# Causal and neighbourhood attention: two softmax blocks added, transposed once, and masked apart again

## The chip, the cores and the metric

The kernel runs on one core of a Trainium2 chip. The metric is the time of one execution on the device in microseconds; of the kernel before, three runs gave 1100.22, 1100.55 and 1100.86 us (median 1100.55).

## The reference, cut to what matters

Three layers work on a sequence of 512 tokens with 1024 channels, all in float32: a recurrent layer (RG-LRU), a layer of causal sliding-window attention, and a block that runs two attentions side by side (a two-sided window and a neighbourhood on an 8 x 64 grid) ahead of an MLP. The causal one and the neighbourhood one are touched here.

```python
def sliding_window_sink_attention(q, k, v, sinks):      # 16 heads, 2 key heads, WINDOW = BLOCK = 128
    # each block of 128 queries sees the block of keys before it and its own
    dist = (jnp.arange(BLOCK)[:, None] + BLOCK) - jnp.arange(2 * BLOCK)[None, :]
    valid = (dist >= 0)[None] & (dist < WINDOW)[None] & (abs_k >= 0)
    s = jnp.where(valid, s + alibi, -jnp.inf)
    ...
    p = (p / denom); o = einsum('bnkgqs,bnskd->bnqkgd', p, vb)

def neighborhood_attn(q, k, v, rpb):                    # 8 heads, grid of 8 rows x 64 columns
    col_start = jnp.clip(cols - B_KW // 2, 0, GRID_W - B_KW)      # each column sees 16 columns, all 8 rows
    ...
    p = softmax(scores + bias); out = einsum(p, v)
```

In the causal attention a query at place q of its block sees key k of the block before only if k > q, and key k of its own block only if k <= q. So for each query each of the 128 places is seen in exactly one of the two blocks. In the neighbourhood attention, with 16 columns seen and the grid cut into blocks of 16 columns, the same holds column by column, except that for the queries at the two edges of the grid one block is seen whole and the other not at all.

## The kernel before, in words

Activations lie as 128 channels by 512 tokens. All large products run on TensorE as a stream of tiles of 128 x 128 weights against 512 tokens. A float32 product is made of three matmuls of a narrower kind: weights and activations are each split into a high and a low part (ScalarE makes the high part of a weight unit of eight tiles, L1094, and VectorE the low part `wl`, L1414). One tile, three matmuls (L900 to L902), is the unit of time, a tick, in which the whole program is ordered: every piece of work on every engine is a generator that yields the tick at which it wants to be issued, and `merge` writes each engine's pieces out in the order of these ticks. The ticks fix only the order; when something really runs is up to the semaphores it waits for. An engine runs its list strictly in order, so that an instruction that waits holds up all behind it.

Attention is cut into 32 jobs of four heads (or of two heads and two query blocks): 16 causal jobs `s`, 8 windowed jobs `w`, 8 neighbourhood jobs `n`. They are threaded into the projections: `s` into the projection that makes queries and gates of the second layer, `w` and `n` into those of the last block. `SETS` (L552) holds each kind's first tick and the ticks per unit of work, and `plan_steps` (L558) lays out steps. In step n TensorE does the products of job n-3 (`prods`, L1055 or L1049), the scores of job n (L1009) and the turns of job n-2 (L1024), in this order; between the steps run projection tiles. A causal step with two blocks in all its parts is 0.84 x 8 = 6.72 ticks wide, a neighbourhood step 1.6 x 8 = 12.8.

A job of kind `s` or `n` with two key blocks runs like this. VectorE adds the bias to the scores of each of the four heads, with the minimum of the row (`biases`, L1682 for `s`, L1691 for `n`); ScalarE takes the exponential with its sum, in place in a tile `Pt` of 128 queries x 256 keys (L1298); VectorE adds the sink's term and takes the reciprocal (L1711, L1714; L1700 for `n`); GpSimd multiplies the tile by it (`normals`, L1958). TensorE transposes each 128 x 128 half of the four tiles into one PSUM bank, a turn of four transposes for each key block (`turns`). A turn is copied to SBUF (a tile `PT` of 128 keys x 4 x 128 queries) by VectorE if its number is even (L1728) and by ScalarE if it is odd (L1315), both placed 0.2 ticks behind the turn; then `prods` multiplies it with the values. The first causal block has only one key block: 4 of the 16 causal jobs. The next job's scores wait until VectorE has done all four biases of the job before (`bias_done`). Windowed jobs have two or three key blocks that overlap in their places.

Behind the causal stage, `y_mix` (L1651), `y_high` (L1286) and the low part (L1656) build the gated output for the next projection, placed by `y_tick` (L672); the silu of the gates (L1645) runs beside the attention.

Of the kernel before, what the change touches and what calls it, by code (L numbers as in the profile page):

```python
# [279 lines left out]
def build(nc, xT, wst, wcr, par, cst, nbias, wdn, fin, out):  # L280
    ctx = ExitStack()
    with ctx:
        def sem(n):
            return ctx.enter_context(nc.semaphore(n))
# [21 lines left out]
        sums_r = [sb(n, [128, 128], R)[:, :] for n in ("ones_r", "hones_r")]  # L306
        crossw = sb("crossw", [128, 4, 4, 32])
# [94 lines left out]
        fin_in, cross_in, cross_half = sem("fin_in"), sem("cross_in"), sem("cross_half")  # L402

# [123 lines left out]

        def unit_split(q, v):

            q.wait_ge(hi_done, v + 2)  # L530
            q.wait_ge(lo_done, v + 2)
# [3 lines left out]
        jobs, t_no = [], 0  # L535
# [16 lines left out]
        SETS = {"s": (0, 16, A_END + 44.5, 0.84), "w": (16, 24, B_END + 50.3, 1.22), "n": (24, 32, B_END + 145.3, 1.6)}  # L552
# [5 lines left out]
        def plan_steps(kind):  # L558

            a, z, tick, step = SETS[kind]
            at = {}
            for n in range(a, z + 3):
                n_prod = jobs[n - 3]["nk"] if n >= a + 3 else 0
                n_turn = jobs[n - 2]["nk"] if a + 2 <= n < z + 2 else 0
                wide = step * max(5.5 if n < z and kind != "n" else 0, (4 if n < z else 0) + n_turn + n_prod)
                for kb in range(n_prod):
                    at["prod", n - 3, kb] = tick
                for i in range(4 if n < z else 0):  # L570
                    at["score", n, i] = tick + (0.5 * wide if kind == "w" and i > 1 else 0.0)
                for kb in range(n_turn):
# [128 lines left out]
        def _(e):  # L701
# [81 lines left out]
            merge([weights(), starts(), biases(), swaps(), downs(), gains(), stores()])  # L783
# [3 lines left out]
        def _(e):  # L787
# [282 lines left out]
        def _(e):  # L1070
# [205 lines left out]
            def silu_b(c):  # L1276
                yield ev_at["bq", 8 + c] + 0.8
                q.wait_ge(ev_done, ev_no(("bq", 8 + c)))
                q.wait_ge(silu2_done, c - 1)
                e.activation(th_b[c % 2], gu_b[c % 2], ACT.Tanh, scale=0.5).then_inc(th_done, 1)  # L1280

            def y_high(c):
                yield y_tick(c) + 1.0
# [22 lines left out]
            def turn_copies(kind):  # L1306
                for m in range(*SETS[kind][:2]):
                    for kb in range(jobs[m]["nk"]):
                        t = jobs[m]["t0"] + kb
                        if t % 2:  # L1310
                            yield step_at["turn", m, kb] + 0.2
                            o, ring = t_tile(m, kb)
                            q.wait_ge(turn_done, t + 1)
                            q.wait_ge(prod_done, t - ring + 1)
                            e.activation(o, bank[TB[t % 2]], ACT.Copy).then_inc(pta_done, 1)  # L1315
# [82 lines left out]
        def _(e):  # L1398
# [239 lines left out]
            def silu_b(c):  # L1638
# [3 lines left out]
                yield ev_at["bq", 8 + c] + 1.9  # L1642
# [15 lines left out]
            def biases(kind):  # L1658
                for m in range(*SETS[kind][:2]):
                    job = jobs[m]  # L1660
                    w = 128 * job["nk"]
                    for i in range(4):
                        yield score_tick(m, i) + 0.4
# [8 lines left out]
                        if old >= 4 * (0 if kind == "s" else 16):  # L1672
                            o = jobs[old // 4]
                            q.wait_ge(turn_done, o["t0"] + o["nk"])
# [18 lines left out]
                        if i % 2:  # L1693
                            pair = 2 * m + i // 2
                            rd = stat_(m, 3, i - 1, i + 1)
                            if kind == "n":
                                yield score_tick(m, i) + 1.35
# [10 lines left out]
                            yield score_tick(m, i) + 1.35  # L1708
# [10 lines left out]
            def turn_copies(kind):  # L1719
                for m in range(*SETS[kind][:2]):  # L1720
                    for kb in range(jobs[m]["nk"]):
                        t = jobs[m]["t0"] + kb
                        if t % 2 == 0:
                            yield step_at["turn", m, kb] + 0.2
                            o, ring = t_tile(m, kb)
                            q.wait_ge(turn_done, t + 1)
                            q.wait_ge(prod_done, t - ring + 1)
                            e.tensor_copy(o, bank[TB[t % 2]]).then_inc(ptd_done, 1)  # L1728
# [188 lines left out]
        def _(e):  # L1917
# [31 lines left out]

            def normals(kind):  # L1950
                for m in range(*SETS[kind][:2]):
                    w = 128 * jobs[m]["nk"]
                    for i in range(4):
                        yield score_tick(m, i | 1) + 1.6
                        q.wait_ge(rd_done, 2 * m + i // 2 + 1)
                        q.wait_ge(exp_done, 4 * m + i + 1)
                        pm = p_tile(m, i)[0][:, 0:w]
# [17 lines left out]
            lanes += [normals(kind) for kind in SETS]  # L1975
# [163 lines left out]

# [23 lines left out]
```

## Time and profile before

| | |
|---|---|
| median of three runs | 1100.55 us |
| the profiled execution | 1100.17 us |
| its span | 1098.4 us |
| TensorE busy | 1087.8 us, 99% |
| VectorE busy | 753.4 us, 69% |
| ScalarE busy | 551.7 us, 50% |
| GpSimd busy | 121.4 us, 11% |
| granted clock of TensorE | 0.998 of full speed |

The span is from the first to the last instruction; the execution's own time is 1.8 us longer. TensorE's matmuls overlap in the records, so their mean length (390 ns for one of 512 columns) is more than each takes from the stream. The causal stage lies at about 265 to 385 us of the span, the windowed one at 462 to 560 us, the neighbourhood one at 563 to 657 us.

### The profile page before, as it was taken

The numbers are of one execution on the slowest core, as the hardware profiler recorded it, in microseconds if no ns is written. First come the engines' busy times: TensorE is split into PE (matmuls) and PEld (weight loads), VectorE is DVE, ScalarE is ACT, GpSimd is POOL, SyncE is SP. The second block draws the span as 40 slices with busy tenths as digits, with TensorE's granted clock in tenths as the row PEclk, the third lists the DMA queues.
The fourth block names the chain that finished last, engine by engine and source line by source line (L and its number), as shares of the span: only waits on it lengthen the run. The fifth ranks groups of instructions, "written<-read, shape, count | busy, mean of one in ns | idle before, by whom it ended". The sixth has DMA issues, their size and how long they took to land.

```text
span 1098.4 us, 14327 instructions
## 1 busy us (share of the span) xinstructions
PE 1087.8 (99%) x5216; PEld 863.0 (79%) x5216; DVE 753.4 (69%) x1274; ACT 551.7 (50%) x939; POOL 121.4 (11%) x170
## 2 busy tenths in 40 slices
PE   9999999999999999999999999999999999999997
PEld 6787787887677788767778788888888888888886
DVE  7898886777668765365545545546697796796795
ACT  6766656565666544244444433335553453453455
POOL 2000000120223311032112110003000000000003
PEclk9999999999999999999999999999999999999999
DMA  6322322332111222311322212323501702602401
GB/s 232 127 77 96 96 84 70 116 115 87 58 43 67 65 81 96 102 65 63 104 72 100 77 60 96 105 89 121 204 20 60 266 1 74 233 1 84 166 1 77
DMA packets 29910, 103.01 MB, mean 94 GB/s; under 512 B 3472, under 2 KB 3856, under 8 KB 29840
## 3 DMA queue, kind: packets, MB, share of 16 engines
q1 hardware_dynamic: 29408, 101.47, 27.1%
q8 instruction: 42, 0.69, 0.3%
q10 hardware_dynamic: 432, 0.62, 0.2%
q14 instruction: 28, 0.23, 0.1%
HBM read 99.45 MB, written 2.10 MB: 92 GB/s over the span
## 4 chain that ended last, share of the span: by engine, by line
PE 97%; DVE 1%; issue 0%; ACT 0%; POOL 0%; DVEq 0%; POOLq 0%
PE ps L900 24%; PE ps L901 24%; PE ps L902 24%; PE ps L864 4%; PE ps L863 4%; PE ps L865 4%; PE ps L1009 3%; PE ps L1024 3%; PE ps L1055 2%; PE ps L813 1%; PE ps L1049 1%; PE ps L946 0%; PE ps L938 0%; PE ps L965 0%; PE ps L975 0%
## 5 line engine op out<-in xcount | busy, mean ns | idle before, releaser
L900 PE MATMUL ps<-xgh,wh 128*128 128x512 f32 x847 | 336.8, 398 | 1.7 <-ACT trr L1184 0.8
L902 PE MATMUL ps<-xgh,wl 128*128 128x512 f32 x847 | 330.2, 390 | 0.0
L901 PE MATMUL ps<-xgl,wh 128*128 128x512 f32 x847 | 330.0, 390 | 0.0
L1414 DVE TENSOR_TENSOR wl<-raw,wh 128x1024 fp32r<-128x1024 f32 x146 | 186.3, 1277 | 44.4 <-ACT wh L1094 43.7
L1094 ACT ACTIVATE wh<-raw 128x1024 fp32r<-128x1024 f32 x146 | 153.0, 1050 | 78.7 <-PE ps L902 58.2
L900 PEld LDWEIGHTS ps<-xgh,wh 128*128 128x128 f32 x847 | 159.0, 188 | 40.8 <-issue 6.4
L902 PEld LDWEIGHTS ps<-xgh,wl 128*128 128x128 f32 x847 | 159.0, 188 | 33.8
L901 PEld LDWEIGHTS ps<-xgl,wh 128*128 128x128 f32 x847 | 159.2, 188 | 32.2 <-issue 1.0
L1958 POOL TENSOR_SCALAR Pt<-Pt,stat 128x256 f32<-128x256 f32 (+2 forms) x128 | 74.0, 590 | 275.8 <-DVE stat L1714 200.3
L1298 ACT ACTIVATE Pt<-Pt,stat 128x256 f32<-128x256 f32 (+2 forms) x128 | 64.3, 503 | 60.5 <-DVE stat L1682 23.1
L863 PE MATMUL ps<-wh,fh 128*128 128x512 f32 x224 | 87.1, 389 | 0.0
L864 PE MATMUL ps<-wl,fh 128*128 128x512 f32 x224 | 87.1, 389 | 0.0
L865 PE MATMUL ps<-wh,fl 128*128 128x512 f32 x224 | 87.1, 389 | 0.0
L1094 ACT ACTIVATE wh<-b 128x1024 fp32r<-128x1024 f32 x40 | 42.3, 1060 | 50.5 <-PE ps L865 40.5
L1315 ACT ACTIVATE PT<-ps 128x512 f32<-128x512 f32 x32 | 19.1, 597 | 80.2 <-PE ps L1024 80.1
L1890 DVE TENSOR_TENSOR xtok<-ps,xtok 128x512 f32<-128x512 f32 x56 | 38.0, 685 | 26.2 <-PE ps L865 26.2
L1728 DVE COPY PT<-ps 128x512 f32<-128x512 f32 x32 | 22.1, 690 | 49.3 <-PE ps L1024 49.0
L865 PEld LDWEIGHTS ps<-wh,fl 128*128 128x128 f32 x224 | 42.0, 188 | 8.8
L863 PEld LDWEIGHTS ps<-wh,fh 128*128 128x128 f32 x224 | 42.0, 188 | 8.8
L864 PEld LDWEIGHTS ps<-wl,fh 128*128 128x128 f32 x224 | 42.0, 188 | 8.7
L1414 DVE TENSOR_TENSOR wl<-b,wh 128x1024 fp32r<-128x1024 f32 x40 | 48.3, 1215 | 0.1
L1363 ACT ACTIVATE fa<-rl 128x512 f32<-128x512 f32 x32 | 20.1, 627 | 43.1 <-DVE rl L1835 43.1
(239 smaller groups left out, 1656.1 us busy)
## 6 DMA issues: line engine op xcount, KB each, us to landing
raw<-wst SPq DMA_DIRECT2D x146, 512.0 KB, 3.5
b<-wdn SPq DMA_DIRECT2D x32, 512.0 KB, 6.9
bst<-nbias SPq DMA_DIRECT2D x8, 256.0 KB, 3.3
xt<-xT SPq DMA_DIRECT2D x3, 512.0 KB, 7.8
outT<-xtok SPq DMA_DIRECT2D x3, 512.0 KB, 2.6
sq<-fin SPq DMA_DIRECT2D x2, 256.0 KB, 4.3
cstt<-cst SPq DMA_DIRECT2D x1, 448.0 KB, 5.6
raw<-wst SPq DMA_DIRECT2D x1, 320.0 KB, 5.0
```

The source lines that it names most:

```text
L863: e.matmul(o, a, high, start=(k == 0 and not on), stop=False, skip_group_check=on)
L864: e.matmul(o, a, low, start=False, stop=False, skip_group_check=on)
L865: e.matmul(o, b, high, start=False, stop=stop, skip_group_check=on).then_inc(tile_done, 1)
L900: e.matmul(o, high, a, start=(k == 0), stop=False)
L901: e.matmul(o, high, b, start=False, stop=False)
L902: done = e.matmul(o, low, a, start=False, stop=stop)
L1009: e.matmul(score_place(m, i + p), own, seen, start=True, stop=True).then_inc(score_done, 1)
L1094: e.activation(wh_t[:, v % NHL, :], src, ACT.Copy).then_inc(hi_done, 1)
L1298: e.activation(pa, pa, ACT.Exp, scale=-1.0, bias=stat_(m, 0, i, i + 1), accum_out=stat_(m, 1, i, i + 1)).then_inc(exp_done, 1)
L1414: e.tensor_tensor(wl_t[:, v % NHL, :], src, f32(wh_t[:, v % NHL, :]), ALU.subtract).then_inc(lo_done, 1)
L1890: e.tensor_tensor(x_, bank[ch.bank[name]], x_, ALU.add).then_inc(ev_done, 1)
L1958: e.tensor_scalar(pm, pm, stat_(m, 3, i, i + 1), 1.0, ALU.mult, ALU.mult).then_inc(nrm_done, 1)
```

## The change: what it does

For causal jobs with two blocks and for all neighbourhood jobs (`packed`), GpSimd adds the two halves of each `Pt` tile after the exponential (masked places are exactly zero there), normalises 128 columns instead of 256, and TensorE turns the sum once. The two blocks are got back on the keys' side by multiplying the turned tile with two complementary masks of 0 and 1, which come from the host and lie in the room of `crossw`, 256 KB each for the causal and for the neighbourhood kind.

For the neighbourhood jobs VectorE makes both masked tiles straight from PSUM. For the causal jobs ScalarE copies the turned bank to the second tile, VectorE multiplies that into the first tile with the first mask, and when it has, GpSimd multiplies the second tile in place with the other. Jobs that aren't packed are copied as before. Several places in the order move: copies from 0.2 to 1.0 ticks behind the turn, biases 0.4 ticks earlier, reciprocals from 1.35 to 2.15, normalisations from 1.6 to 2.4, the silu and the mixing of the causal stage, and the windowed set from `B_END + 50.3` with 1.22 to `B_END + 52.3` with 1.28. The width of a step still counts both blocks as turns.

```diff
+            job["packed"] = job["kind"] == "n" or (job["kind"] == "s" and job["nk"] == 2)
+            job["turns"] = 1 if job["packed"] else job["nk"]
...
-        SETS = {"s": (0, 16, A_END + 44.5, 0.84), "w": (16, 24, B_END + 50.3, 1.22), "n": (24, 32, B_END + 145.3, 1.6)}
+        SETS = {"s": (0, 16, A_END + 44.5, 0.84), "w": (16, 24, B_END + 52.3, 1.28), "n": (24, 32, B_END + 145.3, 1.6)}
...
-            return max(ev_at["bq", 8 + c] + 2.4, done[c // 4] + 1.4 + (1.1 if c > 3 else 6.0) * (c % 4))
+            return max(ev_at["bq", 8 + c] + 2.4, done[c // 4] + 3.4 + (1.1 if c > 3 else 4.0) * (c % 4))
...
+            def attention_masks():
+                yield end["gi", 11] + 4.0
+                q.wait_ge(tile_done, end["gi", 11] + 1)
+                e.dma_start(masks[:, :, :, :], msk[0]).then_inc(mask_in, 16)
+                yield end["z", 5]
+                copy_done(q, copied[15, 0])
+                if 15 in masked:
+                    q.wait_ge(mask_done, masked[15])
+                q.wait_ge(tile_done, B_END)
+                e.dma_start(masks[:, :, :, :], msk[1]).then_inc(mask_in, 16)
...
             def turns(kind):
                 for m in range(*SETS[kind][:2]):
                     job = jobs[m]
-                    for kb in range(job["nk"]):
+                    for kb in range(job["turns"]):
                         yield step_at["turn", m, kb]
-                        t = job["t0"] + kb
-                        q.wait_ge(pta_done if t % 2 else ptd_done, t // 2)
+                        t = job["u0"] + kb
+                        if t > 1:
+                            copy_done(q, bank_read[t - 2])
...
-                        q.wait_ge(pta_done if t % 2 else ptd_done, t // 2 + 1)
+                        copy_done(q, copied[m, kb])
+                        if kb and m in masked:
+                            q.wait_ge(mask_done, masked[m])
...
-                            yield step_at["turn", m, kb] + 0.2
+                            yield step_at["turn", m, 0 if packed else kb] + 1.0
                             o, ring = t_tile(m, kb)
...
-                            e.activation(o, bank[TB[t % 2]], ACT.Copy).then_inc(pta_done, 1)
+                            e.activation(o, bank[TB[u % 2]], ACT.Copy).then_inc(pta_done, 1)
...
-                        yield score_tick(m, i) + 0.4
+                        yield score_tick(m, i) + 0.0
...
-                            yield score_tick(m, i) + 1.35
+                            yield score_tick(m, i) + 2.15
...
+                        yield step_at["turn", m, 0 if packed else kb] + (2.6 if packed else 1.0)
...
+                        turned = bank[TB[u % 2]]
+                        if m in masked:
+                            copy_done(q, copied[m, 1])
+                            turned = t_tile(m, 1)[0]
...
+                            wide, seen = "p (b q) -> p b q", masks[:, kb, 0, :].unsqueeze(1).to_broadcast([128, 4, 128])
+                            e.tensor_tensor(o.rearrange(wide, b=4), turned.rearrange(wide, b=4), seen,
+                                            ALU.mult).then_inc(ptd_done, 1)
...
+            def packs(kind):
+                for m in range(*SETS[kind][:2]):
+                    for i in range(4 if jobs[m]["packed"] else 0):
+                        yield score_tick(m, i) + 1.9
+                        q.wait_ge(exp_done, 4 * m + i + 1)
+                        pm = p_tile(m, i)[0]
+                        e.tensor_tensor(pm[:, 0:128], pm[:, 0:128], pm[:, 128:256], ALU.add).then_inc(pack_done, 1)
+
+            def second_masks(kind):
+                for m in range(*SETS[kind][:2]):
+                    if m in masked:
+                        yield step_at["turn", m, 0] + 2.0
+                        o = t_tile(m, 1)[0]
+                        copy_done(q, copied[m, 1])
+                        copy_done(q, copied[m, 0])
+                        q.wait_ge(mask_in, 16 if kind == "s" else 32)
...
+                            o = o.rearrange(wide, b=4)
+                        e.tensor_tensor(o, o, seen, ALU.mult).then_inc(mask_done, 1)
+
             def normals(kind):
                 for m in range(*SETS[kind][:2]):
-                    w = 128 * jobs[m]["nk"]
+                    w = 128 * jobs[m]["turns"]
                     for i in range(4):
-                        yield score_tick(m, i | 1) + 1.6
+                        yield score_tick(m, i | 1) + 2.4
```

## Rows read from the trace of the kernel before

**Rows 1.** The page: busy time of each engine, then the chain's shares by engine.
```profile
PE 1087.8 (99%) x5216; PEld 863.0 (79%) x5216; DVE 753.4 (69%) x1274; ACT 551.7 (50%) x939; POOL 121.4 (11%) x170
...
PE 97%; DVE 1%; issue 0%; ACT 0%; POOL 0%; DVEq 0%; POOLq 0%
```

**Rows 2.** Waits of TensorE, 265 to 386 us: total us, times, longest.
```profile
PE ps L1009 <- DVE stat L1682: 0.6, 1, 0.6
```

**Rows 3.** Groups by line and form, TensorE: count, busy us, mean ns, idle before.
```profile
L1024 PE MATMUL ps<-cstt,Pt 128*128 128x128 f32 x256 | 35.9, 280 | 0.0
```

**Rows 4.** The chain in order of time, causal stage: start us, us, what.
```profile
335.01 0.59 PE ps L1024 x4
...
345.36 0.58 PE ps L1055 x4
...
354.22 1.02 PE ps L1024 x8
...
355.25 0.23 PE ps L900
...
360.04 1.01 PE ps L1055 x8
...
380.95 1.02 PE ps L1024 x8
...
384.05 1.01 PE ps L1055 x8
```

**Rows 5.** The chain in order of time, neighbourhood stage.
```profile
585.08 1.02 PE ps L1024 x8
```

**Rows 6.** Groups by line and form, VectorE and ScalarE, 240 to 386 us.
```profile
L1414 DVE TENSOR_TENSOR wl<-raw,wh 128x1024 fp32r<-128x1024 f32 x17 | 20.8, 1221 | 1.0 <-ACT wh L1094 0.8
...
L1656 DVE TENSOR_TENSOR y2l<-sgt,y2h 128x512 fp32r<-128x512 f32 x4 | 2.8, 689 | 0.2 <-ACT y2h L1286 0.2
...
L1315 ACT ACTIVATE PT<-ps 128x512 f32<-128x512 f32 x14 | 8.3, 596 | 17.0 <-PE ps L1024 16.9
```

**Rows 7.** GpSimd's operations: two lines' durations (ns min/median/max), and one in order of time.
```profile
L1948 POOL TENSOR_TENSOR ssq<-ssq,sq x21: 1325/1342/1853, 210.0 to 764.6; 128x512 f32<-128x512 f32 x21
...
L1958 POOL TENSOR_SCALAR Pt<-Pt,stat x64: 365/478/1891, 269.0 to 376.9; 128x256 f32<-128x256 f32 x48, 128x128 f32<-128x128 f32 x16
...
396.34 0.65 POOL L1945 TENSOR_SCALAR ssq<-sq 128x512 f32<-128x512 f32 x1 [18.49 <-ACT sq L1228]
```

**Rows 8.** Busy us (xcount) by stretch: length, PE, PEld, DVE, ACT, POOL; clock, DMA.
```profile
345.30:375.10 29.80, 29.80 (x173) 22.07 (x172) 23.16 (x74) 19.09 (x56) 11.88 (x17) 1.00 0.18 60
...
265.00:385.00 120.00, 119.30 (x672) 86.34 (x671) 84.98 (x285) 76.01 (x221) 34.95 (x64) 1.00 0.18 58
560.00:680.00 120.00, 120.00 (x673) 96.03 (x672) 60.73 (x138) 51.47 (x108) 17.67 (x32) 1.00 0.25 84
```

**Rows 9.** DMA issues: count, KB each, us from issue to landing.
```profile
crossw<-wcr SPq DMA_DIRECT2D x1, 256.0 KB, 4.3
```

**Rows 10.** VectorE in order of time, a dense causal step: start us, us, instruction.
```profile
358.19 0.16 DVE L1711 TENSOR_TENSOR stat<-stat 128x2 f32<-128x2 f32 x1 [0.69 <-ACT stat L1304]
...
359.58 0.47 DVE L1682 CUSTOM_DVE_ANT_0 Pt<-ps,cstt,drv 128x256 f32<-128x256 f32 x1
359.99 0.07 DVE L1682 DVE_READ_ACCUMULATOR2_ANT stat<- 128x1 f32 x1
```

**Rows 11.** VectorE and GpSimd in order of time, two places.
```profile
353.50 1.20 DVE L1414 TENSOR_TENSOR wl<-raw,wh 128x1024 fp32r<-128x1024 f32 x1
354.62 0.68 DVE L1656 TENSOR_TENSOR y2l<-sgt,y2h 128x512 fp32r<-128x512 f32 x1
...
353.67 2.34 POOL L1958 TENSOR_SCALAR Pt<-Pt,stat 128x256 f32<-128x256 f32 x2 [1.27 <-DVE stat L1714]
...
398.98 1.32 POOL L1948 TENSOR_TENSOR ssq<-ssq,sq 128x512 f32<-128x512 f32 x1 [1.99 <-ACT sq L1228]
...
399.08 2.31 DVE L1414 TENSOR_TENSOR wl<-raw,wh 128x1024 fp32r<-128x1024 f32 x1
```

More of the change, by code:

```diff
@@ L526, in form_no_, with copy_done @@
             return n + ({"A11": 1, "A": 2, "S": 3} if k == KH - 1 else {"A11": 1, "A": 1, "S": 2})[part]
+        def copy_done(q, which):
+            q.wait_ge(pta_done if which[0] == "act" else ptd_done, which[1])
         def unit_split(q, v):
@@ L534, in build @@
         D1, D2 = C_("D1"), C_("D2")
-        jobs, t_no = [], 0
+        jobs, t_no, u_no, pack_no = [], 0, 0, 0
+        copies, copied, bank_read = {"act": 0, "dve": 0}, {}, {}
+        masked, masks_no, SHARED = {}, 0, ('s',)
         for g in range(2):
@@ L551, in build @@
             t_no += job["nk"]
-        SETS = {"s": (0, 16, A_END + 44.5, 0.84), "w": (16, 24, B_END + 50.3, 1.22), "n": (24, 32, B_END + 145.3, 1.6)}
+            job["packed"] = job["kind"] == "n" or (job["kind"] == "s" and job["nk"] == 2)
+            job["turns"] = 1 if job["packed"] else job["nk"]
+            job["u0"], job["packs"] = u_no, pack_no
+            u_no += job["turns"]
+            pack_no += 4 * job["packed"]
+            for kb in range(job["nk"]):
+                u = job["u0"] + (0 if job["packed"] else kb)
+                by = ("dve", "act")[kb if job["packed"] and job["kind"] in SHARED else 0 if job["packed"] else u % 2]
+                copies[by] += 1
+                copied[m, kb] = (by, copies[by])
+                if by == "act" or not (job["packed"] and job["kind"] in SHARED):
+                    bank_read[u] = copied[m, kb]
+                if job["packed"] and by == "act":
+                    masked[m] = masks_no = masks_no + 1
+        SETS = {"s": (0, 16, A_END + 44.5, 0.84), "w": (16, 24, B_END + 52.3, 1.28), "n": (24, 32, B_END + 145.3, 1.6)}
         def head(job, i):
@@ L571, in plan_steps @@
                     at["score", n, i] = tick + (0.5 * wide if kind == "w" and i > 1 else 0.0)
-                for kb in range(n_turn):
+                for kb in range(jobs[n - 2]["turns"] if n_turn else 0):
                     at["turn", n - 2, kb] = tick + (0.5 * wide if kb > 1 else 0.0)
@@ L781, in stores @@
                 q.wait_ge(out_done, 16 * 5)
-            merge([weights(), starts(), biases(), swaps(), downs(), gains(), stores()])
+            merge([weights(), starts(), attention_masks(), biases(), swaps(), downs(), gains(), stores()])
         @block.tensor
@@ L1673, in biases @@
                             o = jobs[old // 4]
[L1674 removed]
+                            q.wait_ge(turn_done, o["u0"] + o["turns"])
                         if m >= 2:
@@ L1722, in turn_copies @@
                         t = jobs[m]["t0"] + kb
[L1723 to L1728, printed above, removed]
+                        if copied[m, kb][0] == "act":
+                            continue
+                        packed = jobs[m]["packed"]
+                        yield step_at["turn", m, 0 if packed else kb] + (2.6 if packed else 1.0)
+                        o, ring = t_tile(m, kb)
+                        u = jobs[m]["u0"] + (0 if packed else kb)
+                        q.wait_ge(turn_done, u + 1)
+                        q.wait_ge(prod_done, t - ring + 1)
+                        if not packed:
+                            e.tensor_copy(o, bank[TB[u % 2]]).then_inc(ptd_done, 1)
+                            continue
+                        q.wait_ge(mask_in, 16 if kind == "s" else 32)
[3 more added lines that the diff above has]
+                            turned = t_tile(m, 1)[0]
+                        if kind == "n" and jobs[m]["half"]:
+                            wide, seen = "p (a b q) -> p a b q", masks[:, kb, :, :].unsqueeze(2).to_broadcast([128, 2, 2, 128])
+                            e.tensor_tensor(o.rearrange(wide, a=2, b=2), turned.rearrange(wide, a=2, b=2), seen,
+                                            ALU.mult).then_inc(ptd_done, 1)
+                        else:
+                            wide, seen = "p (b q) -> p b q", masks[:, kb, 0, :].unsqueeze(1).to_broadcast([128, 4, 128])
+                            e.tensor_tensor(o.rearrange(wide, b=4), turned.rearrange(wide, b=4), seen,
+                                            ALU.mult).then_inc(ptd_done, 1)
             def key_a():
@@ L2137, in neighbour_bias, with attention_masks @@
     return full
+def attention_masks():
+    key, own = np.arange(128)[:, None], np.arange(128)[None, :]
+    first = np.stack([np.stack([key > own] * 2), np.stack([key % 16 >= own % 16, (own % 16 < 8) & (key >= 0)])])
+    both = np.stack([first, ~first], axis=1)
+    return np.ascontiguousarray(both.transpose(0, 3, 1, 2, 4).astype(np.float32))
 def kernel(**inputs):
```

31 lines of the change are left out of this document (23 added, 8 removed).

## The prediction

> **What bounds the kernel now.** I read the page first: TensorE is busy in 99% of the span and holds 97% of the chain that ended last [rows 1]. So the end moves when TensorE's own stream gets shorter or when TensorE is made to wait, and by nothing else. Next the list of TensorE's waits: in the attention stages it waits once, 0.6 us, for VectorE's bias step at L1682 [rows 2]; every other hand-over arrives in time. Then the group of the transposes, x256 [rows 3], and the chain in order of time, because groups of matmuls overlap in the busy rows and the chain gives what each really takes from the stream: a run of eight transposes 1.02 us, a run of four 0.59 us, one matmul of the projections 0.23 us [rows 4]. A tick of the written order is one projection tile, three matmuls, 0.69 us.
>
> **What is removed from TensorE.** A turn is four transposes of one 128-key block. Twelve of the sixteen causal jobs (all but the first block's four) and all eight neighbourhood jobs have two blocks; each now has one turn. That is 20 turns, 80 of the 256 transposes. Every such run goes from eight to four: 1.02 - 0.59 = 0.43 us, in the causal stage [rows 4] and the same in the neighbourhood stage [rows 5]. 20 x 0.43 = 8.6 us. The total of the group bounds it from above: 35.9 us / 256 x 80 = 11.2 us [rows 3], but that busy time overlaps its neighbours. The lower bound is 0, if TensorE had been waiting anyway and the wait only grew; with one wait of 0.6 us in the stage [rows 2] that is far off. I take 8.6, measured on the same runs of four and eight. Scores and products stay as they are.
>
> **What is added elsewhere, and what hides it.**
> ScalarE and VectorE in the causal stage: 14 copies each before; after, ScalarE makes 12 + 2 and VectorE 12 masks + 2 copies. A copy on ScalarE is 0.60 us; a VectorE product of 128x512 with both inputs in SBUF is 0.69 us [rows 6], what its copies cost too, so neither engine's load changes by itself.
> GpSimd in the causal stage: 48 sums of 128x128, 12 masks of 128x512, and 48 normalisations at half the width. The mask has a row: 1.34 us [rows 7]. The sum has none. Bounds: 0.37 us (the shortest one-input operation, the 128-wide one) and 1.34 us. The second input of a 128x512 operation costs 1.34 - 0.65 = 0.69 us [rows 7], a quarter of it 0.17, so I take 0.37 + 0.17 = 0.54 us. The normalisation falls from 0.48 (median) to 0.37. A causal step gains 4 x 0.54 + 1.34 - 4 x 0.11 = 3.1 us of GpSimd. In the four steps of 345.3 to 375.1 it was busy 11.9 of 29.8 us [rows 8]; it becomes some 24 of 28.
> Neighbourhood stage: VectorE masks both tiles straight from PSUM, 16 operations for 8 copies, +8 x 0.69 = 5.5 us; it was busy 60.7 of 120 us there [rows 8] and a step holds 12.8 ticks, 8.8 us of tiles. ScalarE loses 8 copies. GpSimd gets 4 x 0.54 a step. TensorE needs the masked tiles a step later, 8.8 us, against 1.4 us for two masks. Cost 0; without that cover it would be 1.4 us a step.
> Two loads of masks, 256 KB each: a load of this size landed in 4.3 us [rows 9]. The first is issued on SyncE behind the last cross gates' tile, 128 ticks (88 us) before the causal stage begins; the weights queued behind it are asked for 40 tiles (27 us) ahead of use. Cost 0; uncovered, 4.3 us each.
> Windowed attention: no work changes; its set starts 2 ticks later with 5% longer steps, so that its last products come 6.3 ticks later, still 6 ticks (4.3 us) ahead of the first tile that reads them, and the copy and the low part after them take 0.60 + 0.69 us. Cost 0, at most 1 us. The widths of the causal and neighbourhood steps in ticks are unchanged: the planner still counts two turns.
>
> **The first cost: the mask chain at the end of the causal stage.** Before, both copies ran side by side behind the turns. Now they are a chain: ScalarE copy 0.60, VectorE mask 0.69, GpSimd mask in place 1.34, together 2.63 us, and by my estimate 2.8 with three hand-overs. In a full step TensorE works 4.8 us between turns and products (355.24 to 360.04) and 0.58 us more on the first block's product before it needs the second tile: 5.4 us, cover 2.6. In the last step only 2.1 us lie between (381.97 to 384.05) [rows 4], 2.7 with the first product; the one before has 3.4. There the chain is on the path: between 0.1 us and, if each of the three engines is busy with one thing of about a microsecond when its turn comes, 3 us over both. I take 0.5.
>
> **The second cost: VectorE in the dense steps.** The next scores wait for all four bias steps of the job before. At 359.58 the last one starts, done at 360.06; the scores follow the products at 361.05 [rows 4, 10]. Cover 1.0 us. The change takes 0.43 us of it by shortening the step, moves the third and fourth bias behind the reciprocal (2.85 ticks, where they stood at 2.05 and 2.5: up to 0.5 us), and puts the mask ahead of them where a copy stood; it fills a 0.69 us hole in which VectorE waited for ScalarE [rows 10], which gives as much back. That alone would be even. What isn't in it is GpSimd. At 353.67 two normalisations, 2 x 0.48 at the median [rows 7], took 2.34 us, next to two VectorE operations with both inputs in SBUF; at 399.08 a weight split that otherwise takes 1.22 us took 2.31, next to a GpSimd sum that had begun 0.10 us before [rows 6, 11]. The split ended 1.1 us after that sum: it stood still until GpSimd was through. With GpSimd going from 35 of 120 us [rows 8] to some 65, VectorE will stand more often. Bounds a step: 0, and 1.1 + 0.4 = 1.5 us. Of the twelve masked steps I count six dense (where the silu and the mixing lie too), at 0.25 us: 1.5 us.
>
> The Trainium skill (SBUF — State Buffer, section "Who interferes with whom") says that a VectorE instruction with two SBUF inputs and a GpSimd instruction that reads SBUF exclude each other, and that the later one waits for the whole of the earlier. Both collisions above agree. By this rule the causal masks on VectorE are of the blocking kind while the old copies from PSUM were not. Taken at its word for every pair it gives the second rival; if the rule did not bear on this kernel, the sum would be near the first rival's.
>
> **Sum.** -8.6 + 0.5 + 1.5 = -6.6 us. The profiled execution took 1100.17 us with a span of 1098.4, so 1093.6 us with a span of 1091.8. The median of the runs shown, 1100.55, lies 0.38 above; between the two I say 1093.8.
>
> **Rivals.**
> 1. No stalls. The chain of 2.8 us just fits, and VectorE absorbs GpSimd's turns in its holes (it is busy 85 of 120 us, [rows 8]). Then the full 8.6 us: 1091.6 to 1091.9. For it: one wait of 0.6 us in all before. Against it: that wait was for exactly this bias step.
> 2. The interface that VectorE and GpSimd share becomes the bound of the causal stage. Four dense steps have 28.1 us. GpSimd 24 us, and VectorE's two-input work there (three splits of 1.22, eight of the silu and mixing kind of about 0.7, the small sums, 4 masks of 0.69) near 15: 39 us if none may overlap. Only some of GpSimd's time can hold the interface, so the excess of 11 us is an upper end; a quarter to two thirds of it gives 3 to 7 us of waiting, and the time 1094.6 to 1098.6. The forecast stalls are this rival's small form; it begins above 3 us.
> 3. Slower than before: TensorE stands at the second tile's product in every masked step. The place is the wait for GpSimd's mask; the price is the chain's excess over 5.4 us. If VectorE reaches the mask as late as it reached its biases in the dense steps (about 2 us behind), the split of 1.22 us lies ahead of it, and a GpSimd sum and a collision of 1.1 us come on top, the chain is 2.8 + 2 + 1.2 = 6.0 to 7.1. It decides from 8.6 / 12 = 0.72 us a step; at 1.0 to 1.5 it costs 12 to 18 us and the time is 1104 to 1110. Against it: the mask stands at 2.6 ticks, ahead of the reciprocal and the later biases, and GpSimd's at 2.0, before most of its sums.
> 4. The change isn't felt, because the removed transposes ran beside something: excluded by the chain, in which four or eight of them make 0.43 us of TensorE's stream; only the loss of cover in w or in the loads (1 us, 4.3 us) could act, worth 1095 to 1098. I put it with the second.
>
> **Chances.** Forecast (stalls of 1 to 3 us, 1092.6 to 1094.9) 0.38; no stalls 0.34; rivals 2 and 4, 0.20; rival 3, 0.08. The range takes in the first rival with 0.9 us to spare and reaches to 1098.3 through most of the second: 1091.0 to 1098.3. A measurement of this kernel can tell about 0.2%, 2.2 us: faster by more than that is all of the forecast and the first rival and seven tenths of the second, 0.86; same 0.08, slower 0.06.
>
> **What would show it.** Right: the transposes x176, runs of four at 0.59 us everywhere in the causal and neighbourhood stages; the neighbourhood stage shorter by 8 x 0.43 = 3.4 us with no TensorE wait; sums on GpSimd of 0.5 to 0.6 us; the causal stage shorter by 5.2 us less TensorE's waits there. The waits' rows name the step: L1009 waiting for the bias step or the products (L1055) waiting for GpSimd's mask. Wrong: VectorE's total in the causal stage up by several microseconds (rival 2), a wait of TensorE on the mask in each step (rival 3), or a run of four transposes that takes much more or less than 0.59 us.

## The result, and the profile after

The changed kernel takes 1093.26 us (median of 4 runs, 1092.70 to 1093.85) against 1100.38 us for the kernel before; the ratio is 0.9935, 95% interval 0.9919 to 0.9951. Forecast was 1093.8 with 1091.0 to 1098.3. The profiled execution has a span of 1091.4 us, 7.0 less than before.

The page of the changed kernel, beside [rows 1]: busy time by engine, and the chain by engine.
```profile
PE 1079.4 (99%) x5136; PEld 854.9 (78%) x5136; DVE 763.4 (70%) x1282; ACT 545.9 (50%) x931; POOL 173.2 (16%) x262
...
PE 93%; DVE 3%; issue 1%; ACT 1%; POOL 1%; DVEq 0%; POOLq 0%
```
TensorE has 80 instructions less. GpSimd (POOL) now has 1% of the chain that ended last, where its share was under half a percent. TensorE's waits of over 0.3 us, the whole execution, beside [rows 2] (engine and line that waited, what for, us in total, times, longest):
```profile
PE ps L1093 <- POOL PT L2030: 2.1, 3, 0.8
PE ps L981 <- POOL ssq L1980: 1.3, 1, 1.3
PE ps L935 <- ACT wh L1121: 0.9, 1, 0.9
PE ps L935 <- ACT trr L1222: 0.8, 1, 0.8
PE ps L997 <- DVE sql L1658: 0.4, 1, 0.4
```
The first is new: the second causal product (L1093, L1055 before) waits three times for GpSimd's mask (L2030). The wait for VectorE's bias step is gone from these rows. The other four lie ahead of the attention; those at 1.3, 0.8 and 0.4 were there before, and the one of 0.9 us differs from kernel to kernel in the traces (none with the neighbourhood only, 1.6 with the masks by VectorE), as does the start of the causal stage, 264.8 to 265.9 us.

The chain in order of time, causal and neighbourhood stage, beside [rows 4, 5] (start us, us, what), and the group of the transposes, beside [rows 3]:
```profile
302.45 0.59 PE ps L1060 x4
...
358.94 0.59 PE ps L1060 x4
```
```profile
581.20 0.59 PE ps L1060 x4
...
592.76 0.59 PE ps L1060 x4
```
```profile
L1060 PE MATMUL ps<-cstt,Pt 128*128 128x128 f32 x176 | 27.1, 284 | 0.0
```
Every run of eight of the jobs that are added has become a run of four at 0.59 us. Where the time went is read best from stretches between the same instructions in both traces, starts of TensorE's groups (the first bound as the chain has it, the other two as the instructions' records have them, in every kernel alike):

| stretch | before | after | difference |
|---|---|---|---|
| up to the first causal scores | 265.18 | 265.56 | +0.38 |
| from there to the last causal products | 118.80 | 114.53 | -4.27 |
| from there to the last neighbourhood products | 271.23 | 268.16 | -3.07 |
| from there to the end | 443.16 | 443.14 | -0.02 |

The last causal wait (0.68 us) lies in the third stretch, since it comes between the two halves of those products. In GpSimd's and VectorE's groups of the causal stage (240 to 384 us; beside [rows 6, 7]; count, busy us, mean ns, idle before) stand the sums, the normalisations and the masks, and two of VectorE's additions of 128x2:
```profile
L2014 POOL TENSOR_TENSOR Pt<-Pt 128x128 f32<-128x128 f32 x48 | 31.7, 666 | 12.5 <-ACT Pt L1336 12.1
L2042 POOL TENSOR_SCALAR Pt<-Pt,stat 128x128 f32<-128x128 f32 x64 | 27.6, 443 | 39.2 <-DVE stat L1754 39.2
L2030 POOL TENSOR_TENSOR PT<-PT,masks 128x512 f32<-128x512 f32 x12 | 15.7, 1310 | 17.3 <-DVE PT L1785 16.0 <-issue 1.3
```
```profile
L1785 DVE TENSOR_TENSOR PT<-PT,masks 128x512 f32<-128x512 f32 x12 | 8.8, 736 | 4.0 <-ACT PT L1355 3.9
L1751 DVE TENSOR_TENSOR stat<-stat 128x2 f32<-128x2 f32 x32 | 8.7, 273 | 6.9 <-ACT stat L1342 6.7
L1746 DVE TENSOR_TENSOR stat<-stat,part 128x2 f32<-128x2 f32 x32 | 8.3, 259 | 0.8
```
The additions took 5.0 and 5.9 us before. Busy time in the two stretches of [rows 8] (length; PE, PEld, DVE, ACT, POOL):
```profile
265.00:385.00 120.00, 117.85 (x638) 83.67 (x637) 93.11 (x288) 77.06 (x224) 74.00 (x124) 1.00 0.18 58
560.00:680.00 120.00, 120.00 (x656) 95.55 (x655) 67.55 (x148) 50.38 (x104) 30.23 (x64) 1.00 0.26 84
```
GpSimd went from 35 to 74 us in the first, VectorE from 85 to 93. The stretch to 385 us holds three more of VectorE's instructions than before, since the stage now ends earlier; between the first causal scores and the last causal products the same 285 instructions took 84.7 us before and 91.1 now, 6.4 us more. In the second stretch TensorE still never stands.

### The profile page after: what moved, and what is told of

Read it like the earlier page. It is cut to its first block, busy times and chain, and to the rows that moved or that the text cites. A ratio compares the mean times of both kernels' runs of the same rounds, so it can differ in the third digit from the quotient of the medians.

```text
span 1091.4 us, 14274 instructions
## 1 busy us (share of the span) xinstructions
PE 1079.4 (99%) x5136; PEld 854.9 (78%) x5136; DVE 763.4 (70%) x1282; ACT 545.9 (50%) x931; POOL 173.2 (16%) x262
## 4 chain that ended last, share of the span: by engine, by line
PE 93%; DVE 3%; issue 1%; ACT 1%; POOL 1%; DVEq 0%; POOLq 0%
PE ps L935 24%; PE ps L937 23%; PE ps L936 23%; PE ps L900 4%; PE ps L898 4%; PE ps L899 4%; PE ps L1044 3%; PE ps L1060 2%; PE ps L1093 2%; PE ps L848 1%; PE ps L1087 1%; DVE Pt L1722 1%; PE ps L981 0%; POOL PT L2030 0%; ACT Pt L1336 0%
## 5 line engine op out<-in xcount | busy, mean ns | idle before, releaser
L2042 POOL TENSOR_SCALAR Pt<-Pt,stat 128x128 f32<-128x128 f32 (+2 forms) x128 | 62.4, 500 | 139.0 <-DVE stat L1754 137.4
L2014 POOL TENSOR_TENSOR Pt<-Pt 128x128 f32<-128x128 f32 x80 | 48.7, 613 | 66.7 <-ACT Pt L1336 66.0
L2050 POOL TENSOR_TENSOR xtok<-xtok,sq 128x512 f32<-128x512 f32 x4 | 5.9, 1507 | 314.4 <-ACT ssq L1179 314.4
```

The costliest lines, as they stand in the source:

```text
L2014: e.tensor_tensor(pm[:, 0:128], pm[:, 0:128], pm[:, 128:256], ALU.add).then_inc(pack_done, 1)
L2042: e.tensor_scalar(pm, pm, stat_(m, 3, i, i + 1), 1.0, ALU.mult, ALU.mult).then_inc(nrm_done, 1)
```

## The experiments

Each is compared with the kernel before, run on the same chip (medians 1100.40, 1100.56 and 1100.76 us on the three chips). The changed kernel stood at 0.9935 of it. "Waits" are TensorE's, from each kernel's profile; the causal stretch is the one of the table above, 118.80 us before. Differences of a few tenths between two changed kernels are read from these stretches, not from medians of different chips.

| kernel | median us | ratio, 95% interval | causal stretch us | waits for a mask |
|---|---|---|---|---|
| changed | 1093.26 | 0.9935 [0.9919, 0.9951] | 114.53 | 2.1, 3 times |
| neighbourhood only | 1095.48 | 0.9954 [0.9938, 0.9971] | 117.83 | none |
| causal only | 1096.87 | 0.9967 [0.9954, 0.9980] | 114.53 | 2.1, 3 times |
| order only | 1099.10 | 0.9987 [0.9978, 0.9997] | 117.83 | none |
| masks by VectorE | 1091.45 | 0.9917 [0.9902, 0.9931] | 113.42 | none |
| small mask | 1090.29 | 0.9907 [0.9893, 0.9922] | 112.69 | none |
| mask twice | 1103.97 | 1.0029 [1.0019, 1.0040] | 124.76 | 8.8, 6 times |
| small sums | 1091.76 | 0.9919 [0.9904, 0.9934] | 113.09 | 0.9, 2 times |
| first mask from PSUM | 1092.96 | 0.9930 [0.9915, 0.9945] | 115.03 | GpSimd's 0.2, VectorE's 0.9 |
| three jobs by VectorE | 1091.19 | 0.9916 [0.9900, 0.9933] | 113.58 | none |
| masks by VectorE, late | 1104.52 | 1.0037 [1.0023, 1.0052] | 126.48 | 9.8, 10 times |
| windowed set only | 1100.97 (one run) | | 118.79 | none |

**The two halves of the change.**
```diff
-            job["packed"] = job["kind"] == "n" or (job["kind"] == "s" and job["nk"] == 2)
+            job["packed"] = job["kind"] == "n"
```


> Only the neighbourhood jobs are added and turned once; the causal jobs are turned twice as before, but keep the moved places in the order. Stream theory (TensorE's stream sets the time): eight turns less, 8 x 0.43 = 3.4 us, so 3.4 us under the kernel before, some 1097.0 us, no wait of TensorE between 560 and 660 us. Rival (the moved places in the order, not the shorter stream, made part of the gain): more than 1 us away from that, under 1096 or over 1098.

Measured: 5.1 us under the kernel before, where eight shorter runs make 3.4. The rival held: 1.7 us are more than the shorter runs give.

With `job["kind"] == "s" and job["nk"] == 2` in that line:

> Only the causal jobs are added and turned once; the neighbourhood jobs are turned twice with plain copies. Stream theory: twelve turns less, 5.2 us, less some 2.1 us of waits for GpSimd's second mask at the products; 3.4 us over the changed kernel, some 1096.7 us, with the same three waits. Rival (GpSimd's and VectorE's shared interface costs beyond the waits that are listed): the causal half gives under 2.5 us, 1098 us or more.

Measured: 1096.87, 3.7 us under the kernel before, the same three waits. As expected for the sum; but these 3.7 us hold the moved places too. Over order only (below) it is 2.2 us.

**The order alone.** `packed` is false for every job.

> The changed kernel with no job added and turned once: only the moved places in the order (copies, biases, reciprocals, normalisations, silu, mixing, the windowed set) and the two loads of masks are left. The neighbourhood-only kernel gave 5.1 us, 1.7 more than eight shorter runs. Theory: that 1.7 us is the moved places, and shows here alone: 1098.7 to 1099.3 us. Rival: it belongs to the neighbourhood stage's new operations, and this kernel takes 1100.4 us like the one before.

Measured: 1099.10, 1.7 us under by the medians (0.3 to 2.4 by the interval), 1.8 by the spans of the profiled executions. By stretches, with 0.37 us of those 1.8 from a different start of the program: the causal one 118.80 to 117.83, the one behind it 271.23 to 270.81. So the moved places give 0.97 + 0.42 = 1.4 us. The causal part comes at the biases: counted from the start of the stage, the third scores begin 0.33 us sooner than before and the fourth 0.62 us more, and from there on the two traces run parallel. Which of the moved places does it is not isolated. The weight loads (PEld) show TensorE waiting for the biases more plainly than the matmul rows, whose ends are modelled. Before, 265 to 386 us:
```profile
PEld ps L1009 <- DVE stat L1682: 1.5, 2, 1.0
```
Order only, 264 to 392 us:
```profile
PEld ps L1044 <- DVE stat L1722: 0.8, 2, 0.5
```
VectorE's own idle time ahead of the additions that wait for ScalarE (L1711, then L1751; 265 to 385 us) is 17.9 us before, 10.3 with order only and 6.9 in the changed kernel.

**The 0.42 us behind the causal stage.** The kernel before, with one edit:
```diff
-"w": (16, 24, B_END + 50.3, 1.22)
+"w": (16, 24, B_END + 52.3, 1.28)
```


> The kernel before with only the windowed set moved (2 ticks later, steps 5% longer). In the traces of the order-only and the neighbourhood-only kernels the stretch behind the causal stage is 0.4 to 0.5 us shorter than the shorter turns explain, and TensorE changes from projection tiles to attention and back 32 times there, not 35. Theory: runs that meet save the change, so the stretch from the last causal products to the last neighbourhood products falls from 271.23 us to 270.8. Rival: it is the copies' and biases' places, and it stays at 271.2.

Measured (one run, and its trace): the stretch is 272.09 us, longer, since one transpose of values waits 1.1 us for VectorE there (`PE ps L975 <- DVE th L1763: 1.1, 1, 1.1`). But TensorE's 1413 instructions of this stretch stand in the same order as in order only, and each starts at the same distance from the start of the stretch within 0.01 us, up to that one place, where this kernel falls some 1.28 us behind and stays so: 272.09 - 1.28 = 270.81, order only's time. So the 0.42 us are the windowed set's, as the theory has it, and the other moved places keep that one wait away. Attention comes in between the projection tiles 33 times in both, 35 times before (not 32, as I had expected).

**Is it GpSimd's mask?** The mask on 4 columns of 512; the rest of the second tile stays unmasked:
```diff
-                        e.tensor_tensor(o, o, seen, ALU.mult).then_inc(mask_done, 1)
+                        e.tensor_tensor(o[:, :, 0:1], o[:, :, 0:1], seen[:, :, 0:1], ALU.mult).then_inc(mask_done, 1)
```


> The changed kernel with GpSimd's second causal mask on 4 columns instead of 512 (the rest of the second tile stays unmasked); the wait on it stays. Chain theory: its 1.3 us fall to some 0.4, the three waits of TensorE (0.60, 0.83, 0.68) go, 1091.2 us. Interface theory: over that, VectorE's short additions get shorter and the time falls below 1090.8. If the waits are VectorE's lateness and not GpSimd's length, they stay above half and the time is over 1092.3.

Measured: 1090.29, 3.0 us less than the changed kernel. The mask takes 0.23 us, no wait is left, and the causal stretch is 112.69, 5.14 us under order only: the twelve shorter runs, whole.

Step by step the two traces also tell what a wait costs. They run parallel within 0.06 us but for the three waits, where the changed kernel falls 0.83, 1.05 and 0.90 us behind, 2.8 us in all; their rows say 0.60, 0.83 and 0.68, together 2.1. A row counts from the recorded end of the matmul before, and that lies some 0.2 us behind the moment at which the next one starts when nothing waits (the first four products are recorded at 0.65 us; unhindered, the fifth starts 0.48 us after the first). With 0.34 us of an earlier start of the program this makes the 3.0 us. So nothing is left for the interface theory in its time, 1090.29. Of its mark there is little: one of VectorE's two kinds of additions of 128x2 stays at 0.27 us on average, the other falls from 0.26 to 0.21.

The same mask applied twice, the second behind the first:
```diff
+                        e.tensor_tensor(o, o, seen, ALU.mult).then_inc(mask_twice, 1)
+                        q.wait_ge(mask_twice, masked[m])
                         e.tensor_tensor(o, o, seen, ALU.mult).then_inc(mask_done, 1)
```


> The changed kernel with GpSimd's second causal mask applied twice in a row, the second waiting for the first: 12 more operations of 1.3 us, each in the chain behind a turn. Cover theory (a full step has 5.4 us for a chain of about 2.8; only where the cover is gone does TensorE wait): the three steps that wait now wait 1.3 us longer each, some other dense steps begin to wait, +4 to +8 us, 1097 to 1101 us. Third rival of the prediction (the mask is on the path of every masked step): +1.3 us in each of twelve, 1109 us.

Measured: 1103.97, 10.7 over the changed kernel, between the two theories' times. But the waits agree with the cover: six of twelve steps wait, 8.8 us in all, 6.7 more than in the changed kernel, and the first four steps still don't (their products come up to 0.3 us late, which no row names). Of the other 4 us, 3.2 are TensorE's clock; the rest is what the rows of the waits leave out. TensorE's order of time, mask twice, around the longest wait:
```profile
350.36 0.65 PE L1093 MATMUL ps<-PT,V 128*64 128x256 f32 x4
353.80 0.65 PE L1093 MATMUL ps<-PT,V 128*64 128x256 f32 x4 [2.79 <-POOL PT L2032]
354.38 1.83 PE L1044 MATMUL ps<-ke,q 64*128 64x256 f32 x8
356.14 1.11 PE L1060 MATMUL ps<-cstt,Pt 128*128 128x128 f32 x4
```
And the stretches around it and around a second wait, of 2.64 us (the column before the last two is the granted clock):
```profile
340.00:350.00 10.00, 10.00 (x54) 7.71 (x53) 9.75 (x28) 7.82 (x22) 6.38 (x11) 1.00 0.16 52
...
354.00:358.00 4.00, 4.00 (x19) 2.66 (x16) 2.34 (x6) 1.71 (x4) 3.25 (x8) 0.58 0.31 118
358.00:362.00 4.00, 4.00 (x19) 3.33 (x18) 3.45 (x12) 1.94 (x7) 2.85 (x4) 0.99 0.00 0
...
384.00:388.00 4.00, 2.71 (x10) 1.85 (x11) 0.00 (x0) 0.57 (x2) 1.14 (x1) 0.67 0.00 0
```
After standing for 2.8 us TensorE ran on at a granted clock of 0.58 for some 4 us, near the lower of its two levels (1.2 of 2.4 GHz): scores of 1.83 us for 1.13, transposes of 1.11 for 0.66. Beyond the wait itself, the steps behind it took 1.6 us longer than in the small mask's kernel, and 1.6 us again behind the second. The three waits of the changed kernel, 0.60 to 0.83 us, cost no clock, nor did the four shorter ones here (up to 1.33 us): the granted clock is 1.00 behind them.

**Do the sums matter?** The causal sums on 2 of 128 columns:
```diff
-                        e.tensor_tensor(pm[:, 0:128], pm[:, 0:128], pm[:, 128:256], ALU.add).then_inc(pack_done, 1)
+                        w = 2 if kind == "s" else 128
+                        e.tensor_tensor(pm[:, 0:w], pm[:, 0:w], pm[:, 128:128 + w], ALU.add).then_inc(pack_done, 1)
```


> The changed kernel with GpSimd's sums of the causal halves on 2 columns instead of 128 (the rest of the two blocks is not added there); the neighbourhood sums stay. Chain theory: the sums are not in the chain behind a turn, so the waits for the second mask stay but for the part that queueing behind the sums adds: 1092.3 to 1093.3 us. Interface theory (the 48 sums cost because they shut VectorE out): VectorE's additions of 128x2 fall from 0.27 to about 0.2 us on average and the time to under 1091.8 us.

Measured: 1091.76, 1.5 under the changed kernel, at the border of the two. The wait at job 10 is gone, the others are 0.2 and 0.7 us. The additions fell from 0.27 to 0.22 us, and from 0.26 to 0.23. So the sums do cost, and the chain theory was too simple; how much of it comes through the queue in which the mask stands and how much through VectorE being held up, this kernel doesn't tell apart.

**A shorter chain on the same engines.** VectorE's first mask reads the turned bank in PSUM, still behind ScalarE's copy; GpSimd starts right behind that copy, beside VectorE:
```diff
                             copy_done(q, copied[m, 1])
-                            turned = t_tile(m, 1)[0]
...
                         copy_done(q, copied[m, 1])
-                        copy_done(q, copied[m, 0])
...
-                            copy_done(q, bank_read[t - 2])
+                            for which in bank_read[t - 2]:
+                                copy_done(q, which)
```


> The changed kernel, but VectorE takes the first causal mask's input from the turned bank in PSUM (behind ScalarE's copy) and GpSimd masks the second tile right behind ScalarE's copy, beside VectorE. The same operations; the chain before the second product falls from 2.6 to 1.9 us, and VectorE's mask has only one input in SBUF. Chain theory: the waits of 0.60, 0.83 and 0.68 us shrink by 0.7 each, 1091.2 to 1091.8 us. If the waits come from GpSimd being busy or shut out when the copy is ready, they stay, 1093 us.

Measured: 1092.96, 0.3 under: nearly nothing. GpSimd's wait falls from 2.1 to 0.2 us, as the chain theory has it, and two others come in its place:
```profile
PE ps L1093 <- DVE PT L1784: 0.9, 2, 0.8
...
PE ps L1043 <- DVE stat L1722: 0.7, 1, 0.7
...
PE ps L1093 <- POOL PT L2028: 0.2, 1, 0.2
```
The reason is in the order of time. Ahead of TensorE's wait of 0.8 us for VectorE's mask, a tiny addition on VectorE (L1746), that otherwise takes 0.16 us, lasts until GpSimd's mask is through, and the low part and VectorE's own mask stand behind it:
```profile
346.96 1.74 POOL L2028 TENSOR_TENSOR PT<-PT,masks 128x512 f32<-128x512 f32 x1
...
347.47 1.25 DVE L1746 TENSOR_TENSOR stat<-stat,part 128x2 f32<-128x2 f32 x1
348.65 0.68 DVE L1696 TENSOR_TENSOR y2l<-sgt,y2h 128x512 fp32r<-128x512 f32 x1
349.25 0.68 DVE L1784 TENSOR_TENSOR PT<-ps,masks 128x512 f32<-128x512 f32 x1
```
The late bias step, at 343.38, goes back to an earlier mask in the same way: the silu at 327.25 took 1.37 us, 0.69 in the changed kernel, beside GpSimd's mask of 326.78, and VectorE carried these 0.65 us along to that step.

**Both masks by VectorE.** `SHARED = ()`, so that the causal jobs are masked like the neighbourhood jobs:

> The changed kernel with both causal masks made by VectorE straight from PSUM, as for the neighbourhood jobs; ScalarE copies and GpSimd masks nothing there. The chain behind a turn shrinks from about 2.8 to 1.4 us, and VectorE gets 12 more operations of 0.68 us. Chain theory (the length of the chain ScalarE, VectorE, GpSimd makes the waits of 2.1 us): these go, VectorE's 8 us fit into its holes since its collisions with GpSimd go too, 1091.2 to 1092. Rival (VectorE is the next bound of the dense causal steps): TensorE waits for VectorE's biases or masks instead, the same time as the changed kernel, 1093.3, or up to 1096.

Measured: 1091.45, as the chain theory says: no wait for a mask, though VectorE makes 24 masks of 0.68 us. The causal stretch is 113.42, still 0.7 over the small mask's; bias steps come late there (weight loads wait 2.6 us for them in five places).

**Only where it waited.** `shared = job["kind"] == "s" and m not in (10, 14, 15)` in the choice of the copying engine.

> The changed kernel, but the three jobs whose products waited for GpSimd (10, 14 and 15) have both masks made by VectorE from PSUM; the other nine stay shared. Local theory (the waits belong to these three places, two of them the short steps at the end): all of the 2.1 us go, with nothing late in their place, 1090.9 to 1091.5 us. Rival: the wait at job 10 moves to another dense step or to VectorE's bias steps, 1091.8 to 1092.6 us.

Measured: 1091.19. The mask waits go; two of 0.3 us for a bias step come. Its median is 2.1 us under the changed kernel's, and it can't be told from all masks on VectorE (causal stretches 113.58 and 113.42).

**The masks out of the biases' way.** Both masks on VectorE, at 4.4 ticks instead of 2.6 (last two jobs 1.0):

> Both causal masks by VectorE from PSUM, and placed 4.4 ticks behind the turn, after the four bias steps (1.0 for the last two jobs), where the kernel with both masks by VectorE had them at 2.6. That kernel still had weight loads waiting 2.6 us in five places for bias steps. Order theory: these waits go, as the masks have 5.4 us of room and need 1.4: 0.4 to 1.0 us under it, 1090.4 to 1091.0 us. Load theory (VectorE has too much to do in the dense steps, wherever the masks stand): no gain, 1091.4 us or more.

Measured: 1104.52, 13 us slower than with the masks at 2.6. Both theories are wrong; ten products wait, 9.8 us in all, the longest 2.8, and the clock falls again (0.90 in 350 to 360). VectorE in order of time with the masks late, one step:
```profile
289.62 0.15 DVE L1746 TENSOR_TENSOR stat<-stat,part 128x2 f32<-128x2 f32 x1
290.04 0.16 DVE L1751 TENSOR_TENSOR stat<-stat 128x2 f32<-128x2 f32 x1 [0.27 <-ACT stat L1342]
...
292.05 0.42 DVE L1751 TENSOR_TENSOR stat<-stat 128x2 f32<-128x2 f32 x1 [0.66 <-ACT stat L1342]
292.50 0.17 DVE L1754 RECIPROCAL stat<-stat 128x2 f32<-128x2 f32 x1
292.59 1.27 DVE L1785 TENSOR_TENSOR PT<-ps,masks 128x512 f32<-128x512 f32 x2
```
The same step with the masks at 2.6 ticks:
```profile
289.83 0.15 DVE L1746 TENSOR_TENSOR stat<-stat,part 128x2 f32<-128x2 f32 x1
289.90 1.28 DVE L1785 TENSOR_TENSOR PT<-ps,masks 128x512 f32<-128x512 f32 x2
291.10 0.15 DVE L1751 TENSOR_TENSOR stat<-stat 128x2 f32<-128x2 f32 x1
```
There the masks begin 2.7 us earlier, and the additions behind them find ScalarE's result ready: 0.27 us of standing is filled. Placed late, the masks stand behind two round trips to ScalarE and two more of the job's bias steps, and TensorE waits for them. How the 13 us divide among waits, clock and late weight loads was not worked out.

## Why the prediction was right, point by point

**What is removed from TensorE, -8.6 us: right.** Runs of four at 0.59 us in both stages. Neighbourhood: the kernels with and without it differ in the stretch from the last causal products to the last neighbourhood products by 270.81 - 267.28 = 3.53 us (order only, neighbourhood only) for 3.44. Causal: 5.14 us for 5.16 once nothing waits (small mask).

**The first cost, the mask chain, 0.5 us: too small; it is 2.1 us by the rows of the waits and 2.8 of TensorE's stream, as the small mask shows.** The place was right for two of the three waits: the last two steps, 0.83 and 0.68 (1.05 and 0.90 of the stream). GpSimd in order of time, changed kernel:
```profile
373.26 2.21 POOL L2042 TENSOR_SCALAR Pt<-Pt,stat 128x128 f32<-128x128 f32 x2
375.45 1.26 POOL L2030 TENSOR_TENSOR PT<-PT,masks 128x512 f32<-128x512 f32 x1
379.70 1.58 POOL L2030 TENSOR_TENSOR PT<-PT,masks 128x512 f32<-128x512 f32 x1 [2.99 <-DVE PT L1785]
```
VectorE beside it:
```profile
373.15 1.23 DVE L1454 TENSOR_TENSOR wl<-raw,wh 128x1024 fp32r<-128x1024 f32 x1 [0.18 <-ACT wh L1132]
374.29 0.69 DVE L1785 TENSOR_TENSOR PT<-PT,masks 128x512 f32<-128x512 f32 x1
```
Two normalisations that take 0.37 each alone took 2.21 us beside a split and the first mask, so that GpSimd was free for its mask only at 375.45, half a microsecond after the first mask had ended. In the last step nothing queued; the chain of 2.6 us, 0.3 us of collision with the silu and 0.4 us of hand-overs were simply more than the room, some 2.5 us from the end of the turn to the second product. The third wait, 0.60 us at 349.73, is in a dense step to which I gave 2.6 us of cover: VectorE reached the first mask at 347.50, some 3 us behind the turn, after three operations of silu and mixing. This is the start of rival 3, in one step of twelve.

**The second cost, VectorE's collisions with GpSimd making the biases late, 1.5 us: not there.** From the start of the causal stage to the scores before the first wait the changed kernel takes 77.23 us; order only, less six shorter runs, 79.80 - 2.58 = 77.22. VectorE was held up, but in time in which it had been waiting for ScalarE: the idle time ahead of its second additions fell from 10.3 to 6.9 us. TensorE's weight loads wait 1.3 us for biases, against 0.8 with order only and 1.5 before, and by the matmul rows its scores no longer wait at all.

**The moved places, put at nothing: they give 1.4 us.** I had let the later biases and the filled hole cancel out, and had given the windowed set a cost of 0 to 1 us. Order only shows 0.97 us in the causal stage and 0.42 behind it, the latter from the windowed set.

**The total was close by luck.** I took 0.5 + 1.5 = 2.0 us off the 8.6. Measured by the stretches are 2.78 for the masks, -1.39 for the moved places, +0.38 for a later start of the program, which no term had, and -0.14 left over, together 1.6. A term that was several times too small, one that wasn't there and one put at nothing hide each other.

**What is added elsewhere: right where it is hidden.** The sum of 128x128 takes 0.46 us at the median (forecast 0.54) but 0.67 on average in the causal stage, the mask 1.29 (1.34), the normalisation 0.37 at the median and 0.44 on average. VectorE's neighbourhood masks cost nothing, and the mask loads landed in 3.6 us with no wait for them.

**Rival 2, the shared interface: it works, but mostly on VectorE.** VectorE's total in the causal stage went up 6.4 us without more work, the mark that I had named; its additions of 128x2, never over 0.27 us before, took up to 0.96 us. But VectorE had that much room; none of TensorE's waits in the attention stages of the changed kernel is for VectorE. The Trainium skill's rule (SBUF — State Buffer, section "Who interferes with whom"), that a VectorE instruction with two SBUF inputs and a GpSimd instruction reading SBUF exclude each other whole, agrees with the 2.21 us above and with the first mask from PSUM, where an addition of 0.16 us stood through GpSimd's mask.

**Rival 1, no stalls,** is what the small mask shows to be possible and three jobs on VectorE come near to. **Rival 3** had its time, 1104 and 1104.5 us, with one more mask in the chain and with the masks behind the biases; its mechanism, a wait for GpSimd's mask in every step, only in part: six of twelve steps wait in the one, and ten in the other, there for VectorE's masks.

## What to carry to other kernels

Price an operation taken off the bounding engine by runs of it in the chain, not by the busy row (0.107 us a transpose, not 0.14). When a hand-over that was one step becomes a chain over three engines, look at the shortest distance between producer and consumer, at the tail of a pipeline, and give at least those instances the short chain. A place in an in-order queue can weigh more than the work itself: the same masks at another place cost 13 us. Test the order without the change: here it was worth 1.4 of 7 us. And take the cost of a wait from the distance between the same starts in two traces; the rows of these three waits were 0.2 us short each.

## What the runs showed of the hardware

- TensorE that stood 2.6 to 2.8 us came back at a granted clock of 0.58 and 0.67 over the next 4 us; having stood up to 1.33 us it kept 1.00. A long wait costs more than itself, here 1.6 us more on each of the two.
- Tiny VectorE operations with both inputs in SBUF can stand for much longer than they take beside a busy GpSimd: 128x2 additions of 0.16 us took up to 0.96 in the changed kernel and 1.25 with the first mask from PSUM. VectorE's masks that read the turned bank in PSUM took 0.67 to 0.69 us each in three kernels; those that read it from SBUF up to 1.02.
- GpSimd's addition of 128x128 takes 0.46 us at the median; on 2 columns 0.20, and 0.37 on average beside VectorE.
